# Low parts of the first three down tiles ahead of the last gate products, and residual rows loaded one by one

## The reference, cut to what matters

```
def _swiglu(h, w_gate, w_up, w_down):
    return (jax.nn.silu(h @ w_gate) * (h @ w_up)) @ w_down

x = x + FFN_HALF * _swiglu(_rmsnorm(x, ffn1_norm[l]), ffn1_w_gate[l], ffn1_w_up[l], ffn1_w_down[l])
...
x = x + FFN_HALF * _swiglu(_rmsnorm(x, ffn2_norm[l]), ffn2_w_gate[l], ffn2_w_up[l], ffn2_w_down[l])
```

## Time and profile before

| | us |
|---|---|
| median of three runs | 2934.89 |
| lowest and highest | 2932.85, 2935.57 |
| the profiled execution | 2934.28 |
| its span, first to last instruction | 2932.5 |

### The profile page before, as it was taken

One profiled execution on the slowest core, in us unless ns is written; L12 is line 12 of the kernel. 1 busy time (PEld: TensorE's weight loads), 2 busy tenths in 40 slices (PEclk: granted clock), 3 DMA queues, 4 the chain that ended last, 5 costly groups with the idle time before them and its releaser, 6 DMA issues.

```text
span 2932.5 us, 35986 instructions
## 1 busy us (share of the span) xinstructions
PE 2750.5 (94%) x14166; PEld 2270.2 (77%) x14166; DVE 1460.7 (50%) x1465; ACT 893.2 (30%) x1379; POOL 1513.6 (52%) x927
## 2 busy tenths in 40 slices
PE   4999999999999998998999999998897999999996
PEld 2788887888788877777777778888785888887885
DVE  7644434233456535777777655443356344444323
ACT  6333233232000112443444332113434333223221
POOL 5888785133694624555555434331046787783130
PEclk9999999999999999998999999999998999999998
DMA  2222224344862554334333254113021222215343
GB/s 97 72 84 86 83 83 187 131 149 147 322 239 93 188 193 147 110 103 142 101 106 103 72 212 158 50 58 129 0 86 54 83 87 83 86 60 211 119 137 117
DMA packets 154980, 349.52 MB, mean 119 GB/s; under 512 B 11724, under 2 KB 63180, under 8 KB 147808
## 3 DMA queue, kind: packets, MB, share of 16 engines
q1 hardware_dynamic: 131744, 284.20, 29.0%
q10 hardware_dynamic: 23104, 63.47, 5.7%
HBM read 257.89 MB, written 89.70 MB: 119 GB/s over the span
## 4 chain that ended last, share of the span: by engine, by line
PE 72%; issue 9%; POOL 7%; DVE 6%; DMA 2%; ACT 2%; ACTq 1%; SPq 0%; POOLq 0%; DVEq 0%
PE G L1152 9%; PE G L1154 8%; PE G L1153 8%; PE G L1042 8%; PE G L1043 7%; PE G L1044 7%; PE G L1214 6%; PE G L1216 6%; PE G L1215 5%; PE G L1249 2%; POOL AL L923 2%; POOL blo L973 1%; PE G L1534 1%; PE G L1286 1%; DMA zrw_d<-po 1%
## 5 line engine op out<-in xcount | busy, mean ns | idle before, releaser
L973 POOL TENSOR_TENSOR blo<-braw,bhi 128x512 fp32r<-128x512 f32 x308 | 434.4, 1440 | 31.2 <-ACT bhi L1671 24.3
L1005 POOL TENSOR_TENSOR whi<-raw,zero 128x1024 fp32r<-128x1024 f32 x63 | 122.7, 1948 | 459.3 <-PE G L1044 375.2
L988 POOL TENSOR_TENSOR blo<-braw,bhi 128x512 fp32r<-128x512 f32 x88 | 142.1, 1624 | 345.6 <-ACT bhi L1827 345.6
L1152 PE MATMUL G<-HT,bhi 128*128 128x512 f32 x704 | 277.1, 394 | 12.1 <-DVE wsum L2369 12.1
L1214 PE MATMUL G<-thi,bhi 128*128 128x512 f32 x704 | 276.3, 392 | 12.2 <-DVE tlo L2444 12.2
L1153 PE MATMUL G<-xlo,bhi 128*128 128x512 f32 x704 | 276.8, 393 | 0.0
L1215 PE MATMUL G<-tlo,bhi 128*128 128x512 f32 x704 | 276.0, 392 | 0.0
L1216 PE MATMUL G<-thi,blo 128*128 128x512 f32 x704 | 275.8, 392 | 0.0
L1154 PE MATMUL G<-HT,blo 128*128 128x512 f32 x704 | 275.6, 391 | 0.0
L1152 PE MATMUL G<-H,bhi 128*128 128x512 f32 x528 | 210.0, 398 | 53.6 <-DVE xlo L2262 28.1
L2444 DVE TENSOR_TENSOR tlo<-traw,thi 128x1024 fp32r<-128x1024 f32 x80 | 107.4, 1360 | 296.1 <-ACT thi L1830 296.1
(11 more groups left out here) (394 smaller groups left out, 5998.2 us busy)
## 6 DMA issues: line engine op xcount, KB each, us to landing
traw<-a_d SPq DMA_DIRECT2D x80, 512.0 KB, 3.6
gw<-gw_d SPq DMA_DIRECT2D x32, 1024.0 KB, 5.3
braw<-in_wg SPq DMA_DIRECT2D x88, 256.0 KB, 2.9
braw<-in_wu SPq DMA_DIRECT2D x88, 256.0 KB, 2.8
a_d<-pr SPq DMA_DIRECT2D x22, 1024.0 KB, 5.3
braw<-in_wd SPq DMA_DIRECT2D x88, 256.0 KB, 3.7
gw_d<-gw SPq DMA_DIRECT2D x16, 1024.0 KB, 4.7
x_park<-xT ACTq DMA_DIRECT2D x16, 512.0 KB, 2.6
```

The source lines that it names most:

```text
L973: tt(lo[:], whole[:], hi[:].bitcast(F32), ALU.subtract).then_inc(signal, n)
L1152: nc.tensor.matmul(dst, wh[:, cols], hi, start=fresh and kk == 0, stop=False, skip_group_check=True)
```

## The change: what it does

`products_made` is cut in two, `first_product` (C11) and the rest. In the last pair of each feed-forward, VectorE makes the low part of tile 0 between `block_adds` and `last_add`, that of tile 1 behind `last_add`, and that of tile 2 behind C11; `down_low` leaves these three out. The rows of blocks 0 to 3 are loaded one each behind the loads of gates 4, 6, 8 and 10, and those of blocks 4 to 7 one each behind gates 34 to 37. The store of the last pair is then issued right behind the loads of gate -1.

```
                 if g == -1:
-                    down_rows(f, range(RC))
                     pair_store(f, PAIRS - 1)
-                if g == step_of(30):
-                    down_rows(f, range(RC, KD))
+                for k in range(RC):
+                    if g == RC + 2 * k:
+                        down_rows(f, range(k, k + 1))
+                    if g == step_of(30) + k:
+                        down_rows(f, range(RC + k, RC + k + 1))
...
-        def products_made(g):
+        def first_product(g):
 
             S = st_dve[1]
             dve.wait_ge(*st_pe[1].at("P2", g))
             dve.wait_ge(*st_dve[0].at("z1", g))
             dve.wait_ge(*S.at("C21", g))
             tt(pr[:, 0, 0:BLK], bank(1, "P2"), gt[:, 0, 0:BLK], ALU.mult).then_inc(*S.sig("C11"))
+
+        def products_made(g):
+
+            S = st_dve[1]
             tt(pr[:, 0, BLK:T], pr[:, 0, BLK:T], gt[:, 0, BLK:T], ALU.mult).then_inc(*S.sig("p12"))
             tt(pr[:, 1, :], pr[:, 1, :], gt[:, 1, :], ALU.mult).then_inc(*S.sig("p2"))
...
                 gates_made(g)
                 if p or f:
                     block_adds(f, p, 1, pr)
+                    if p == PAIRS - 1:
+                        tile_low(f, 0)
                     last_add(f, p, 1, pr)
+                if p == PAIRS - 1:
+                    tile_low(f, 1)
+                first_product(g)
+                if p == PAIRS - 1:
+                    tile_low(f, 2)
                 products_made(g)
 
+        def tile_low(f, t):
+
+            dve.wait_ge(dn_ahi, f * ATILES + t + 1)
+            tt(tiles_lo[place_of(t)][:], tiles_raw[place_of(t)][:], tiles_hi[place_of(t)][:].bitcast(F32),
+               ALU.subtract).then_inc(dn_alo, 1)
+
         def down_low(f, g):
 
             for t in range(ATILES):
-                if tile_gate(t) == g:
-                    dve.wait_ge(dn_ahi, f * ATILES + t + 1)
-                    tt(tiles_lo[place_of(t)][:], tiles_raw[place_of(t)][:], tiles_hi[place_of(t)][:].bitcast(F32),
-                       ALU.subtract).then_inc(dn_alo, 1)
+                if tile_gate(t) == g and t > 2:
+                    tile_low(f, t)
```

## The result

The changed kernel takes 2918.3 us in the median of five runs (2916.76 to 2923.62), the kernel before 2934.89 in the median of five (2932.73 to 2937.43). The ratio is 0.9949, 95% interval 0.9934 to 0.9963: faster by 15 us, with 11 to 19 in the interval. Forecast were 2923.4, a range of 2920.0 to 2928.5, and a gain of 11.5. The direction and the place were right, and 11.5 lies just inside the measured interval; the median lies 1.7 us under the range.

A forecast was written before the change was run, and what follows sets the result against it. TensorE was taken as the bound, standing still at two seams for VectorE's late-ordered low parts. 2934.28 minus 2 x 4.0 (earlier starts) minus 3.5 (clock), rows 0, gave 2922.8, or 2923.4 as median; range 2920 to 2928.5 us.

The forecast's parts named there:

- The bound: TensorE, busy 94% of the span; VectorE and queue edits pay only where it stands still, waiting for low parts, 12.2 us.
- the two seams: Where gate and up's last block product ends and down products begin, once per feed-forward; TensorE idled about 6.1 us at each.
- Part 1: Three low parts moved up on VectorE: TensorE starts 4.0 us earlier per seam (3.4 to 4.5), leaving a 2.1 us stop.
- Lows 1 and 2, C11 and p2: VectorE work behind tile 0's low part at each seam: beside TensorE's work; worst case a 0.3 us stop at tile 2.
- The Trainium skill's rule: VectorE instructions with two SBUF inputs and GpSimd's SBUF reads exclude each other; by it alone TensorE starts at 479.75.
- Part 2: Half clock behind the stops, costing 2.8 and 2.4 us: one short 1.7 us spell over both seams, 3.5 us gained.
- rivals A: As forecast, one short slow spell or two at the seams: 2923.4 to 2925.1 us; chance 0.50.
- B: Clock never falls at the seams: 13.2 us gained, 2921.7, or 2920.7 with the shortest low 0; chance 0.22.
- the seven other stops: Earlier trace's stops of 2.0 to 3.2 us before a product: five followed by about 0.50 to 0.54 clock, two not.
- Part 3: Row loads spread behind single steps instead of together: value 0, bounds -0.5 to +0.5 us.
- The sum: Profiled 2934.28 minus 2 x 4.0 minus 3.5 gives 2922.8; the median, 0.6 above that execution, gives 2923.4 us.
- the range: Whole time between 2920 and 2928.5 us, from the clock never falling to half clock lasting as long as now.

The follow-up runs named there:

- e10: Changed kernel with only tile 0's low part moved, those of tiles 1 and 2 behind p2 as before; one run, seam times 22.86 and 24.18 us.
- e4: Changed kernel with the eight down products needing no low part of tile 0 put first; median 2918.52 us of 7, ratio 0.9953 to the kernel before.
- e3: Kernel before with 24 extra products filling each stop ahead of the down stage; median 2930.62 us of 12, ratio 0.9993 to the kernel before.
- second execution: The changed kernel run again unchanged, with a second profile; median 2922.77 us of 6, ratio 0.9963 to the kernel before.
- e2: Kernel before with only the row loads spread; median 2933.72 us of 12, ratio 1.0003 to the kernel before.
- e1: Changed kernel with the row loads as before, only the low parts moved; median 2921.21 us of 10, ratio 0.9965 to the kernel before.
- e7: Changed kernel with TensorE held at each seam until the low part of tile 1 is made; one run, seam times 21.71 and 23.97 us.
- e8: Changed kernel with products needing no low part first, tile 1's low part before C21, GpSimd's later splits waiting; median 2913.7 us of 6, ratio 0.9938.

## Why the prediction was right and where it was wrong

**The bound** and the place were right: 14.55 of the 17.5 us between the two profiled executions lie at the two seams.

**Part 1** forecast a stop of 2.1 us, bounds 1.6 and 2.7. Four stops of the changed kernel in two executions are 1.82, 1.13, 1.93 and 2.13. The lower bound was wrong: it held low 0 fixed behind a C22 of 1.69 us, the one of the earlier trace rows, while C22 takes 0.70 when it slips in between two splits. I had used that very row as proof of the alternation and not asked what happens when it is not held. It was worth 0.7 us at the second seam: the two starts came 9.3 us earlier in all where 2 x 4.0 = 8.0 stood in the sum. Lows 1 and 2, C11 and p2 beside TensorE's work, with no stop at tile 1 or 2: right, and e10 and e4 show how near it is, e4 by asking 1.1 us too early. The Trainium skill's rule (SBUF — State Buffer, Who interferes with whom) was right on the lock. By it alone low 0 would end its 1.21 us behind the end of the split, at 479.21; it ended at 479.09.

**Part 2**, the clock, is the term of the sum that was mis-sized most in the profiled execution: one short spell over two seams was forecast; it had none and gained 5.3 us (2.8 + 2.4 by the earlier trace rows) instead of 3.5 (e3's trace shows the same price, 2.8 and 2.5). In the second execution it had two. There the starts gave 8.2 us and the clock 2.0. The 3.5 stands between the two, and the seven other stops of the trace of before had said as much: rivals A and B were both the kernel, in different executions. Taking them as alternatives for the median, when executions differ, was the error. The list of seven was also less telling than it looked. Of the two that were 'not followed', the one at 47.69 says little, as TensorE stood again 1.7 us after it started, for 7.88 us; and the cut at 2.0 us left out shorter stops with half clock behind them, such as 1.31 us at 1670.32 in the same trace.

**Part 3**, the rows: forecast 0. e2 agrees within its interval, 2.3 us faster to 4.4 slower, and the unchanged 222.81 us behind step 3 shows no stop for a row.

**The sum** of 11.5 us (0.39%, a ratio of 0.9961) lies inside both measured intervals, 0.9934 to 0.9963 and 0.9949 to 0.9977. For the profiled execution of the result it is 3.05 us short at the seams alone: 1.3 of the starts (part 1) and 1.8 of the clock (part 2). The 14.55 us of the seams are even more than the largest gain of rival B, 14.2, since B too held low 0 behind a C22 of 1.69. Another 3.0 us of the 17.5 lie outside the seams, where the prediction let nothing change.

What failed with these terms is the last step, **the range**. I made it of the costs at the seams alone, with no allowance for what else differs between executions. The level was not at fault in the result itself: its five runs of the kernel before have the same median, 2934.89. But in the 50 runs beside the experiments that kernel ranges from 2924.72 to 2938.54 with medians near 2932, and the medians of five and six of the changed kernel are 2918.3 and 2922.8. A range of 2920.0 at the low end left no room for that spread. That the second median falls into the range and near 2923.4 is in part luck: it was measured beside a kernel before that stood 2.6 us lower than the level of the sum.

Much of the spread is not at the seams. In the twelve profiled executions of the table, the span less the two seam times runs from 2874.6 us (e1) to 2882.5 (e7), 7.9 us. The records of the runs say what goes with it, the mean granted clock: of the 50 runs of the kernel before, the seven at 0.976 or less took 2935.2 to 2938.5 us, and the nine at 0.980 or more 2924.7 to 2929.6. So the stretches at half clock, behind the many other stops too, differ from execution to execution, and the time goes with them. No run held the clock fixed, so this is a close relation and not a cause shown, and it is not one to one. One of these stretches is absorbed. Before, the stretch from 763.4 stood at 0.54 for 6.6 us and TensorE then stopped for 3.15 at 791.42 without a spell behind it. In the changed kernel there was less of a spell there, a longer wait, and a spell behind it:

```profile
PE G L1044 <- DVEq L2494: 4.9, 1, 4.9
```
```profile
784.40:790.00 5.60, 5.52 (x13) 4.42 (x14) 5.42 (x3) 0.00 (x0) 5.52 (x3) 0.51 0.95 357
```

TensorE resumes 65.7 us behind the last down product before (725.7 to 791.4) and 66.0 in the changed kernel (718.5 to 784.5): that point hangs on other work than TensorE's, so a slow spell ahead of it costs nothing. How much of the spread of 14 us each stop makes was not shown.

## What to carry to other kernels

When TensorE waits for an engine that is not late but in the wrong order, move the operand that TensorE needs first ahead of the work that is needed last, and follow the wait to the next operand: moving one low part alone only cuts the stop in two. Price a stop twice, for its length and for the half clock behind it, and treat the second as a spread, not a choice: a stop shortened to about 2 us still cost one of two executions a spell at each seam, and the profiled one without a stop (e8) had none. Before a range is written in microseconds, allow for the spread of the level itself, and look at the granted clock of each run beside its time.

## What the runs showed of the hardware that was not expected

Stops of TensorE of 1.93 and 2.13 us brought 3.4 us of half clock each, at a place where 1.82 and 1.78 brought none. A VectorE sum of 512 columns with both inputs in SBUF took 0.69 to 0.70 us when it started between two GpSimd splits or 0.15 us before the end of one, 0.95 when 0.4 us of a split were left, and 1.4 to 1.8 when it started near the beginning of one; over the same kernel's executions it does either. The whole time of one kernel moved by 0.47% (2924.72 to 2938.54 us) along with its mean granted clock (0.975 to 0.981).
